# A hybrid RG-LRU and SSD step on one core: first chunk without an incoming state, a fourth new state in a norm bank, an earlier branch output, and a tail in two pieces

## The chip, the cores and the metric

The kernel runs on 1 core of a Trainium2 chip, as one launch. The metric is device microseconds of one execution, taken as the median over runs. A single profiled execution of the kernel before gives all the rows below.

## The reference, cut to what matters

One layer over 640 tokens (512 of a new stream, and 8 running streams of 16 tokens), model width 1024, all in fp32:

```python
x = x + 0.5 * swiglu_1(rmsnorm(x))
u = rmsnorm(x)
P = u @ w_in        # lru_x | lru_gate | ssd_z | ssd_xBC | ssd_dt | gates
a = lru_branch(P) @ w_br_lru                    # conv, RG-LRU scan, GeLU gate
# SSD branch, per group g of 4 (8 heads of 64, state 128), in chunks:
y_diag   = (C B^T * Lmat) @ (x * dt)            # inside a chunk
states_k = decay * states_(k-1) + B^T @ (decay_states * x * dt)
y        = y_diag + (C @ states_in) * exp(A_cs) + D * x   # new streams start from states = 0
b = (rmsnorm_group(y * silu(z))) @ w_br_ssd
x = x + (sigmoid(gA) * a + sigmoid(gB) * b) @ w_out
x = x + 0.5 * swiglu_2(rmsnorm(x))
return rmsnorm(x, norm_final_g), the new conv tails, LRU states and SSD states
```

## The kernel before, in words

The activations lie transposed, features on the partitions: 8 tiles of 128 features by 640 tokens, in two halves of 320 columns. Tokens form five chunks of 128: t = 0 to 3 are the prompt, t = 4 the sampled tokens. Each fp32 product is made of three products of a high and a low part. A **unit** is one 128-wide column tile of a weight matrix: 8 feature tiles x 3 products x 2 halves = 48 matmuls of 128x320 (36 in the last FFN group, which has 6 tiles). For each unit SyncE loads w_raw, ScalarE makes w_hi (`cut_weights`, L1005), VectorE makes w_lo (L1433), and TensorE (`unit`, `products`, L656) sums into pu[0] or pu[1], which alternate by a running number: `open_out(o)` waits until output o-2 has been read ("released") by its reader, mostly VectorE. Two more pairs of banks, pn[0] and pn[1], serve the norms and the SSD work.

Nothing schedules this but the order in the text, one loop per engine; the table FILL and `mixer_order()` give each unit of the mixer its place and number. For each SSD group g = 0..3: four units of x, B or C ("xb"), then for each prompt chunk t: `scores(t)` (transposes of x and B, and C B^T, into pn[0]), a unit beside it, `inner(t)` (L858: xd times lmat), the product with the state that comes in, ht (L876), the chunk's own state (L880, pn[1]), and units behind it. Units named z, gl, gs, bl and br are gates and branch projections; a br unit has two outputs, m = 0 and 1.

After chunk 3 comes the end of the group. TensorE transposes the prompt's state (L886, pn[1]), makes scores(4), one unit (`beside_last`), the old states' transposes (`old_state`, L899, pn[1]), inner(4), then four new sampled states, `new_state(0..3)` (L929: xdd times b_seq), with the units `middle` and `late` between 0, 1 and 2, and the products from the old states (`from_state`, L911) inside those units. All four new states use pu slots and numbers of the running order.

The other engines at that place. ScalarE: `decays(4)` (L1286, exp of lmat), then the prompt state's copy hp_rows (L1311) with its DMA (L1313), then b_tok (L1301), then the units. VectorE: the scan that makes lmat (L1853, `step_sums`), `scores(4)` (cbm L1860, xd L1862, xdd L1863, lmat L1866), then in groups 1 to 3 the second output of the last br unit (L1783 in group 1, L1789 and L1791 in group 2, L1794 in group 3) behind a w_lo cut, the beside_last unit's gate (L1763), later decay_states(1) (L1922), the middle unit, and the late unit's gate gbuf (L1427, or L1750 in group 0), and the adds of the new states (L1930). In groups 1 to 3 the late unit's gate reads gbuf, fetched from gate_spill by a ScalarE DMA (L1224). GpSimd: loads es and da_rep (L545, L551), clears ht, and makes b_seq from b_tok once the hp_rows DMA is done, because the two share memory (L599).

For t = 0 of a prompt group, ht is all zeros, cleared by GpSimd; VectorE multiplies the product with ht by es, adds the inner product, scales ht, and adds the chunk's state (L1874, L1876, L1879, L1883).

The decay sums before the mixer take 10 matmuls of 128x32 (L784, L787) and one of 128x128 (L789).

The tail. VectorE adds the last unit to resid (L1427), ScalarE squares it (L1016), VectorE adds the square to rvar (L1448). TensorE turns resid into rows of tokens by a matmul with a diagonal of the gains, `to_rows` (L969, g_fin), 8 for a chunk, and makes the sum of squares per token (L984). VectorE forms variance and scale (L2033 to L2039, with the root on ScalarE, L1416). Rows leave the banks by ScalarE for t = 0, 2, 4 (L1420) and by VectorE for t = 1, 3 (L2042); SyncE stores each chunk with one DMA of 512 KB (L433).

Of the kernel before, what the change touches and what calls it, by code (L numbers as in the profile page):

```python
# [68 lines left out]
def mixer_order():  # L69
# [3 lines left out]
    for g in range(GROUPS):  # L73
# [14 lines left out]
        yield ("new", g, 3), 0, 1  # L88
# [48 lines left out]
ES_PER = ((NT + 1) // 2 * 32, NT // 2 * 32)  # L137
# [10 lines left out]
dt_v dt_a dt_p after_v da_in0 da_in1 xb_th xb_out z_th ht_zero ssd_p ssd_a ssd_v bseq  # L148
h0_in0 h0_in1 hs_step old_mm old_cp c_split fs_mm fs_cp hs_out0 hs_out1 hp_mm hp_cp hp_out yz yn_hi_done yn_lo_done br_s gl_th gl_out0 gl_out1 gl_in gs_th gs_out
ma_in0 ma_in1 ma_in2 ma_in3 mg_b mg_v mh_done ml_done reload tail_mm tail_cp tails_out gfin fin_a fin_v y_a y_v y_dma""".split()  # L150
# [22 lines left out]
def layer(nc, x_prompt, x_sample, state_lru_conv, state_lru_h, state_ssd_conv, state_ssd_h,  # L173
# [7 lines left out]
    with ctx:  # L181
# [57 lines left out]
        with ExitStack() as sc:  # L239
# [14 lines left out]
            g_fin = sb(sc, "g_fin", [P, KT, P])  # L254
            y_out = sb(sc, "y_out", [P, NT, D_MODEL])
            fin = sb(sc, "fin", [P, 8, NT])

# [62 lines left out]
        fin_at = (pn[1], pu[O_FIN % 2], pu[(O_FIN + 1) % 2], pn[0], pn[1])  # L320
# [23 lines left out]
        def _(sp):  # L344
# [93 lines left out]
        def _(pool):  # L438
# [101 lines left out]
            for g in range(GROUPS):  # L540
# [99 lines left out]
        def _(pe):  # L640
# [36 lines left out]
            def ffn(u, o, ci, x_hi, x_lo, mid_hi, mid_lo, xh0, between, after):  # L677

                cut = ("xh_done", "xl_done", xh0, 0)
                for gi, n, uu, ou, cc, ud, od in ffn_plan(u, o, ci):  # L680
# [15 lines left out]
                    with pe.Fori(0, KT // 2) as i:  # L696
                        for k in range(2):
                            unit(ud + k, od + k, 2, 2, i, mid_hi, mid_lo, n, ready=hidden if k == 0 else None)

# [86 lines left out]
            for t in range(NT):  # L786
                pe.matmul(pn[1][:, 1, (NT + t) * HEADS:(NT + t + 1) * HEADS], le_mask[:, t // (NT - 1), :], da_col[:, t, :],  # L787
                          start=True, stop=True)
# [43 lines left out]
            for g in range(GROUPS):  # L832
# [20 lines left out]
                def inner(t):  # L853
# [6 lines left out]
                    ins.then_inc(s["ssd_p"], 1)  # L860
# [8 lines left out]
                for t in range(NT - 1):  # L869
# [3 lines left out]
                    if t == 0:  # L873
                        pe.wait_ge(s["ht_zero"], g + 1)
# [1199 lines left out]
```

## Time and profile before

| | |
|---|---|
| median of 3 runs | 1873.62 us (1873.21 to 1874.85) |
| the profiled execution | 1874.83 us |
| its span | 1873.1 us |
| TensorE clock granted, mean | 0.996 |
| TensorE busy | 1842.6 us, 98% |
| VectorE, ScalarE, GpSimd busy | 1111.5, 650.2, 141.1 us |

The span is what the profiler saw of the core; 1.7 us of the execution lie around it. TensorE executes nearly all the time, so the views to read are those that show where it does not (its waits by releaser), what runs on it that need not (timeline), and the end, where it has no work left. Each row of a timeline has the start in us, the duration of the (merged) instructions, the engine, the line, the operation, out<-in, the shape and a count; in brackets stands the engine's idle time before it and what ended it.

### The profile page before, as it was taken

How to read it: one execution, taken by the hardware profiler on the slowest of the kernel's cores; microseconds unless marked ns; L12 is line 12 of the kernel's file. 1: busy time of each engine (PE TensorE's matmuls, PEld its weight loads, DVE VectorE, ACT ScalarE, POOL GpSimd, SP SyncE). 2: the span in 40 equal slices, each digit the busy share in tenths (PEclk: the TensorE clock that was granted, in tenths of full speed). 3: DMA queues.
4: the chain of work that ended last, by engine and by line, in shares of the span. 5: the costliest groups of instructions: out<-in, count | busy, mean ns of one | idle time of the engine just before them, and what ended most of it. 6: DMA issues, size and time to landing. Idle time of an engine off the chain costs nothing.

```text
span 1873.1 us, 31253 instructions
## 1 busy us (share of the span) xinstructions
PE 1842.6 (98%) x12623; PEld 1791.3 (96%) x12623; DVE 1111.5 (59%) x1368; ACT 650.2 (35%) x850; POOL 141.1 (8%) x269
## 2 busy tenths in 40 slices
PE   8999999999999999999999999999999999999998
PEld 7999999999989999989989989998999999999998
DVE  6443443345777775777787887886754433442444
ACT  5221332123577742344244235233342212221223
POOL 3000000000011220111111101110200000000000
PEclk9999999999999999999999999999999999999999
DMA  5222222222422253353354335336522222222222
GB/s 148 68 78 73 73 78 71 76 78 59 135 63 80 70 145 110 110 173 92 112 152 119 107 98 168 106 107 214 191 67 79 78 79 68 78 79 68 78 65 81
DMA packets 273342, 186.13 MB, mean 99 GB/s; under 512 B 7452, under 2 KB 260580, under 8 KB 273008
## 3 DMA queue, kind: packets, MB, share of 16 engines
q1 hardware_dynamic: 239840, 129.52, 24.0%
q0 software_dynamic: 10624, 36.91, 6.5%
q10 hardware_dynamic: 22800, 18.62, 3.1%
q8 instruction: 55, 0.90, 0.2%
q14 instruction: 23, 0.19, 0.0%
HBM read 162.48 MB, written 22.53 MB: 99 GB/s over the span
## 4 chain that ended last, share of the span: by engine, by line
PE 86%; DVE 7%; ACT 3%; issue 2%; DMA 1%; ACTq 0%; DVEq 0%
PE pu L656 80%; DMA gbuf<-gate_spill 1%; PE pn L858 1%; PE pn L876 1%; DVE w_lo L1433 1%; PE pn L753 1%; PE pn L880 1%; PE pu L715 0%; DVE bc L1427 0%; PE pn L899 0%; DVE h_b L1922 0%; PE pn L911 0%; PE pn L847 0%; ACT w_hi L1005 0%; DVE squares L1427 0%
## 5 line engine op out<-in xcount | busy, mean ns | idle before, releaser
L1433 DVE TENSOR_TENSOR w_lo<-w_raw,w_hi 128x1024 fp32r<-128x1024 f32 x240 | 296.5, 1235 | 460.3 <-ACT w_hi L1005 458.7
L656 PE MATMUL pu<-act_hi,w_hi 128*128 128x320 f32 x1952 | 456.9, 315 | 6.7 <-DVE xc L1427 2.2
L656 PE MATMUL pu<-act_lo,w_hi 128*128 128x320 f32 x1952 | 446.9, 310 | 1.1 <-DVE act_lo L1476 1.0
L656 PE MATMUL pu<-act_hi,w_lo 128*128 128x320 f32 x1952 | 446.4, 310 | 0.0
L1005 ACT ACTIVATE w_hi<-w_raw 128x1024 fp32r<-128x1024 f32 x240 | 253.5, 1056 | 513.8 <-PE pu L656 512.7
L656 PEld LDWEIGHTS pu<-act_hi,w_hi 128*128 128x128 f32 x1952 | 327.0, 189 | 23.7 <-issue 19.6
L656 PE MATMUL pu<-x_hi,w_hi 128*128 128x320 f32 x1440 | 329.3, 310 | 1.3 <-DVE ff_g L1489 1.3
L656 PEld LDWEIGHTS pu<-act_lo,w_hi 128*128 128x128 f32 x1952 | 328.1, 189 | 2.4 <-DVE act_lo L1476 1.5
L656 PE MATMUL pu<-x_lo,w_hi 128*128 128x320 f32 x1440 | 328.4, 309 | 0.0
L656 PE MATMUL pu<-x_hi,w_lo 128*128 128x320 f32 x1440 | 328.4, 309 | 0.0
L656 PEld LDWEIGHTS pu<-act_hi,w_lo 128*128 128x128 f32 x1952 | 328.3, 189 | 0.0
L656 PEld LDWEIGHTS pu<-x_hi,w_hi 128*128 128x128 f32 x1440 | 240.8, 188 | 2.3 <-DVE ff_g L1489 1.8
L656 PEld LDWEIGHTS pu<-x_lo,w_hi 128*128 128x128 f32 x1440 | 240.7, 188 | 0.0
L656 PEld LDWEIGHTS pu<-x_hi,w_lo 128*128 128x128 f32 x1440 | 240.7, 188 | 0.0
L1286 ACT ACTIVATE lmat<-lmat 128x1024 f32<-128x1024 f32 x20 | 21.2, 1060 | 138.4 <-DVE lmat L1853 138.4
L1044 ACT ACTIVATE act_hi<-ff_h 128x640 f32 (+1 forms) x44 | 32.5, 739 | 94.3 <-DVE ff_h L1496 94.3
L1041 ACT ACTIVATE ff_t<-ff_g 128x640 f32<-128x640 f32 x44 | 32.5, 739 | 92.5 <-DVE ff_g L1489 92.5
L656 PE MATMUL pu<-yn_hi,w_hi 128*128 128x320 f32 x256 | 62.6, 326 | 0.2
L1498 DVE TENSOR_TENSOR act_lo<-ff_h,act_hi 128x640 f32 (+1 forms) x44 | 36.3, 825 | 44.5 <-ACT act_hi L1044 44.5
L656 PE MATMUL pu<-yn_lo,w_hi 128*128 128x320 f32 x256 | 58.4, 310 | 0.0
L656 PE MATMUL pu<-yn_hi,w_lo 128*128 128x320 f32 x256 | 58.2, 309 | 0.0
L1427 DVE SCALAR_TENSOR_TENSOR ff_a<-ff_t,ff_g 128x640 f32<-128x640 f32 x44 | 36.3, 825 | 35.4 <-ACT ff_t L1041 35.4
(323 smaller groups left out, 1883.9 us busy)
## 6 DMA issues: line engine op xcount, KB each, us to landing
w_raw<-in_ffn_w_up_dram SPq DMA_DIRECT2D x87, 512.0 KB, 3.8
w_raw<-in_w_in_dram SPq DMA_DIRECT2D x73, 512.0 KB, 3.9
w_raw<-in_ffn_w_down_dram SPq DMA_DIRECT2D x32, 512.0 KB, 3.7
da_rep<-e_spill POOLq DMA_DIRECT2D x20, 512.0 KB, 4.4
w_raw<-in_w_br_ssd_dram SPq DMA_DIRECT2D x16, 512.0 KB, 3.5
w_raw<-in_ffn_w_down_dram SPq DMA_DIRECT2D x16, 384.0 KB, 3.2
gate_spill<-gbuf ACTq DMA_DIRECT2D x18, 320.0 KB, 2.4
es<-e_spill POOLq DMA_DIRECT2D x40, 128.0 KB, 3.9
```

The costliest lines, as they stand in the source:

```text
L656: ins = pe.matmul(dst[:, h, :], w[:, side, c, :], a[:, k, h * HALF:(h + 1) * HALF], start=(at == 0), stop=(at == n - 1))
L753: ins = pe.matmul(pn[w][:, h, 0:HALF], w_gates[:, w, :], xc[:, h * HALF:(h + 1) * HALF], start=True, stop=True)
L858: ins = pe.matmul(pn[0][r:r + HD, 0, (h // 2) * P:(h // 2 + 1) * P], xd[:, h, :], lmat[:, h, :], start=True, stop=True)
L876: ins = pe.matmul(pn[0][:, 1, q * P:(q + 1) * P], ht[:, 2 * q:2 * q + 2, :].rearrange("n a b -> n (a b)"), xft(g, 5)[:, t * P:(t + 1) * P] ...
L880: pe.matmul(pn[1][:, 1, :], b_tok[:, :], xdd[:, :, :].rearrange("p h d -> p (h d)"), start=True, stop=True).then_inc(s["ssd_p"], 1)
L1005: act.activation(w_hi[:, side, :, :], w_raw[:, side, :, :], ACT.Copy).then_inc(s["w_hi_done"], 1)
L1041: act.activation(ff_t[:, :], ff_g[:, :], ACT.Tanh, scale=0.5).then_inc(s["ff_th"], 1)
L1044: act.activation(feature_tile(mid_hi, i), ff_h[:, :], ACT.Copy).then_inc(s["ff_hi"], 1)
L1286: act.activation(lmat[:, :, :], lmat[:, :, :], ACT.Exp).then_inc(s["ssd_a"], 1)
L1427: return dve.scalar_tensor_tensor(out=dst, in0=a, scalar=scalar, in1=b, op0=op0, op1=op1)
L1433: dve.tensor_tensor(w_lo[:, side, :, :], w_raw[:, side, :, :], w_hi[:, side, :, :].bitcast(F32), ALU.subtract).then_inc(s["w_lo_done"], 1)
L1498: dve.tensor_tensor(feature_tile(mid_lo, i), ff_h[:, :], feature_tile(mid_hi, i).bitcast(F32), ALU.subtract).then_inc(s["ff_lo"], 1)
```

## The change

Six parts. (1) new_state(3) goes into pn[1], with semaphores of its own (ns_mm, ns_v), and its number leaves the running order, so the next unit opens on the late unit's release. (2) At t = 0 TensorE leaves out the matmuls with ht; VectorE copies the inner product to es and the chunk's state to ht; GpSimd no longer clears ht or loads es for t = 0. (3) The decay sums are taken for four chunks in one matmul of 128x128. (4) ScalarE makes the last b_tok ahead of hp_rows and its DMA. (5) VectorE reads the br unit's second output ahead of scores(4), with the w_lo cut behind scores(4), in groups 1 to 3; decay_states(1) goes behind the middle unit and new_state(1). (6) The tail: the last down unit is summed by halves of 320 tokens; ScalarE multiplies resid by the gain as the units arrive (x_gain), so `to_rows` is a transpose and g_fin is gone; the sums of squares, variance, root and scale are made in two pieces (t = 0, 1 and t = 2, 3, 4); ScalarE takes out t = 0, 1, 3 and half of 4, VectorE t = 2 and the other half of 4; the last chunk is stored by two DMAs of 256 KB.

```diff
@@ mixer_order
-        yield ("new", g, 3), 0, 1
@@ tail banks
-        fin_at = (pn[1], pu[O_FIN % 2], pu[(O_FIN + 1) % 2], pn[0], pn[1])
+        fin_at = (pn[1], pu[O_FIN % 2], pn[0], pu[(O_FIN - 1) % 2], pn[1])
+        fin_sums = pu[(O_FIN - 1) % 2][:, 0, HALF:HALF + NT]
@@ SyncE: the last stores
-            for t in range(NT):
-                sp.wait_ge(s["y_v" if t % 2 else "y_a"], t // 2 + 1)
...
+            for t, name, n in ((0, "y_a", 1), (1, "y_a", 2), (2, "y_v", 1), (3, "y_a", 3)):
...
+            for b, name, n in ((0, "y_a", 4), (1, "y_v", 2)):
+                sp.wait_ge(s[name], n)
+                sp.dma_start(y_sample.rearrange("b l d -> (b l) d")[:, b * 512:(b + 1) * 512],
+                             y_out[:, NT - 1, b * 512:(b + 1) * 512]).then_inc(s["y_dma"], 16)
@@ GpSimd, start of a group
-                load_decay(0)
-                pool.memset(ht[:, :, :], 0.0).then_inc(s["ht_zero"], 1)
@@ TensorE: FFN, last down group
-                    with pe.Fori(0, KT // 2) as i:
+                    last = u == U_FFN2 and gi == len(FFN_GROUPS) - 1
+                    with pe.Fori(0, KT // 2 - (1 if last else 0)) as i:
...
+                    if last:
+                        unit(ud + KT - 2, od + KT - 2, 0, 0, 0, mid_hi, mid_lo, n)
+                        last_unit(ud + KT - 1, od + KT - 1, mid_hi, mid_lo, n)
+            def last_unit(u, o, hi, lo, nk):
...
+                for h in range(2):
+                    for k in range(nk):
+                        if h == 1 and k == nk - 1:
+                            token_sums(0)
+                        for w, a in ((w_hi, hi), (w_lo, hi), (w_hi, lo)):
+                            ins = pe.matmul(out(o)[:, h, :], w[:, u % 2, k, :], a[:, k, h * HALF:(h + 1) * HALF],
...
+                    ins.then_inc(s["out_ready" if h else "fin_half"], 1)
@@ TensorE: decay sums
-            for t in range(NT):
-                pe.matmul(pn[1][:, 0, t * HEADS:(t + 1) * HEADS], gt_mask[:, t // (NT - 1), :], da_col[:, t, :],
...
+            for m, chunks in enumerate((slice(0, NT - 1), slice(NT - 1, NT))):
...
@@ TensorE: SSD chunk loop
-                    if t == 0:
-                        pe.wait_ge(s["ht_zero"], g + 1)
-                    for q in range(PAIRS):
-                        ins = pe.matmul(pn[0][:, 1, q * P:(q + 1) * P],
...
+                    if t:
+                        for q in range(PAIRS):
+                            ins = pe.matmul(pn[0][:, 1, q * P:(q + 1) * P],
...
+                    if g and t == 0:
+                        pe.wait_ge(s["ns_v"], g)
@@ TensorE: new_state
-                    o = O_AT["new", g, q]
-                    open_out(o)
+                    if q < PAIRS - 1:
+                        open_out(O_AT["new", g, q])
+                        dst = pu[O_AT["new", g, q] % 2]
+                    else:
+                        dst = pn[1]
...
+                    ins.then_inc(s["out_ready" if q < PAIRS - 1 else "ns_mm"], 1)
@@ TensorE: tail
-            def to_rows(t, k):
-                return pe.matmul(fin_at[t][:, k // 4, (k % 4) * P:(k % 4 + 1) * P], resid[:, k, t * P:(t + 1) * P], g_fin[:, k, :],
...
+            def to_rows(t):
+                for k in range(KT):
+                    ins = pe.transpose(fin_at[t][:, k // 4, (k % 4) * P:(k % 4 + 1) * P], x_gain[:, k, t * P:(t + 1) * P], ident[:, :])
...
+            pe.wait_ge(s["fin_g"], KT)
+            to_rows(0)
+            pe.wait_ge(s["out_free"], O_FIN - 1)
+            to_rows(1)
+            token_sums(1)
+            pe.wait_ge(s["fin_g"], KT + 1)
+            to_rows(2)
+            pe.wait_ge(s["out_free"], O_FIN)
+            pe.wait_ge(s["fin_v"], 6)
+            to_rows(3)
+            pe.wait_ge(s["y_a"], 1)
+            to_rows(4)
@@ ScalarE: last unit by halves, after one x_gain tile with each earlier square
+                        for h in range(2):
...
+                            if h == 0:
+                                act.wait_ge(s["fin_r"], 1)
+                            else:
+                                token_root(0)
+                                act.wait_ge(s["out_free"], O_FIN)
+                            act.activation(squares[:, 1, part], resid[:, KT - 1, part], ACT.Square).then_inc(s["fin_sq"], 1)
+                            act.activation(x_gain[:, KT - 1, part], resid[:, KT - 1, part], ACT.Copy,
...
@@ ScalarE: chunk loop (the four lines of hp_rows move up, behind the last b_tok)
+                    if t == NT - 1:
+                        act.wait_ge(s["hp_mm"], g + 1)
+                        act.activation(hp_rows[:, :, :].rearrange("p q n -> p (q n)"), pn[1][:, 1, :], ACT.Copy).then_inc(s["hp_cp"], 1)
...
-                    if t == NT - 2:
...
@@ ScalarE: tail
+            rows_out(0, 2)
+            token_root(1)
+            rows_out(1, 2)
+            rows_out(3, 2)
+            rows_out(4, 1)
@@ VectorE: outputs of a chunk
+                    if t:
+                        decay_in(t)
...
+                    else:
...
+                        dve.tensor_copy(yv, pn[0][:, 0, :]).then_inc(s["ssd_v"], SV_T2 - SV_G)
...
+                        dve.tensor_copy(hv, pn[1][:, 1, :]).then_inc(s["ssd_v"], SV_H1 - SV_T2)
@@ VectorE: end of a group
-                scores(NT - 1)
-                finish(held[0])
+                if held[0][0] == "br":
+                    branch_out(*held[0][1:], 1, cut=False)
+                    scores(NT - 1)
+                    branch_cut(*held[0][1:])
+                else:
+                    scores(NT - 1)
+                    finish(held[0])
...
-                decay_states(1)
                 fill([middle])
                 new_state(1)
+                decay_states(1)
```

VectorE at the end of group 1, before: the scan, then the four operations of scores(4), a weight cut, and only then the second output of the br unit, acc_ssd.

```order
L1783 TENSOR_TENSOR acc_ssd<-rstd,pu 128x640
L1853 SCALAR_TENSOR_TENSOR lmat<-da_rep,after 128x1024
L1860 TENSOR_TENSOR cbm<-pn,le_mask 128x128
L1862 TENSOR_TENSOR xd<-pn,dt_col 128x512
L1863 TENSOR_TENSOR xdd<-pn,dd_col 128x512
L1866 TENSOR_TENSOR lmat<-lmat,cbm 128x1024
L1433 TENSOR_TENSOR w_lo<-w_raw,w_hi 128x1024
L1783 TENSOR_TENSOR acc_ssd<-rstd,pu 128x640
L1763 TENSOR_SCALAR gbuf<-gbuf 128x640
```

The same place in the changed kernel:

```order
L1861 TENSOR_TENSOR acc_ssd<-rstd,pu 128x640
L1931 SCALAR_TENSOR_TENSOR lmat<-da_rep,after 128x1024
L1861 TENSOR_TENSOR acc_ssd<-rstd,pu 128x640
L1938 TENSOR_TENSOR cbm<-pn,le_mask 128x128
L1940 TENSOR_TENSOR xd<-pn,dt_col 128x512
L1941 TENSOR_TENSOR xdd<-pn,dd_col 128x512
L1944 TENSOR_TENSOR lmat<-lmat,cbm 128x1024
L1481 TENSOR_TENSOR w_lo<-w_raw,w_hi 128x1024
L1838 TENSOR_SCALAR gbuf<-gbuf 128x640
```

The second acc_ssd has moved from behind the cut to ahead of cbm; the cut stays behind scores(4).

TensorE behind the last down unit, before: 7 of the 8 row matmuls of chunks 0 and 1, the last of each, then the sums per token (ones, rvar) inside chunk 2.

```order
L969 MATMUL pn<-g_fin,resid 128x128 x7
L969 MATMUL pu<-g_fin,resid 128x128 x7
L969 MATMUL pn<-g_fin,resid 128x128
L969 MATMUL pu<-g_fin,resid 128x128 x5
L984 MATMUL pn<-ones,rvar 128x1 x5
L969 MATMUL pu<-g_fin,resid 128x128 x4
L969 MATMUL pn<-g_fin,resid 128x128 x16
```

The same place in the changed kernel, from the last feature tile of the second half on:

```order
L709 MATMUL pu<-ones,rvar 128x1 x2
L721 MATMUL pu<-act_hi,w_hi 128x320
L721 MATMUL pu<-act_hi,w_lo 128x320
L721 MATMUL pu<-act_lo,w_hi 128x320
L1000 MATMUL pn<-ident,x_gain 128x128 x8
L1000 MATMUL pu<-ident,x_gain 128x128 x8
L709 MATMUL pu<-ones,rvar 128x1 x3
L1000 MATMUL pn<-ident,x_gain 128x128 x8
L1000 MATMUL pu<-ident,x_gain 128x128 x8
L1000 MATMUL pn<-ident,x_gain 128x128 x8
```

Two of the sums now stand inside the last unit, three behind the rows of chunks 0 and 1.

## Rows read from the trace of the kernel before

**Rows 1.** The page, part 1: busy time, share of the span and instructions.
```profile
PE 1842.6 (98%) x12623; PEld 1791.3 (96%) x12623; DVE 1111.5 (59%) x1368; ACT 650.2 (35%) x850; POOL 141.1 (8%) x269
```

**Rows 2.** TensorE's waits: who waited <- for whom: us in total, times, longest.
```profile
PE pu L929 <- DVE gbuf L1427: 2.9, 3, 1.1
...
PE pu L929 <- DVE squares L1789: 1.6, 1, 1.6
PE pu L656 <- DVE gbuf L1763: 1.6, 3, 0.5
...
PE pu L656 <- DVE gbuf L1750: 1.2, 2, 0.8
...
PE pn L899 <- ACT h_t L1325: 0.8, 2, 0.4
PE pu L929 <- DVE acc_ssd L1783: 0.8, 1, 0.8
...
PE pu L656 <- DVE h_b L1930: 0.4, 1, 0.4
```

**Rows 3.** Chain of waits, last 39 us of TensorE's units: start, us, what.
```profile
1818.96 37.52 PE pu L656 x254
```

**Rows 4.** Timeline of TensorE, first chunk of group 1.
```profile
873.95 1.16 PE L876 MATMUL pn<-bc,ht 128*128 128x128 f32 x8
874.94 0.59 PE L880 MATMUL pn<-xdd,b_tok 128*128 128x512 f32 x1
```

**Rows 5.** Timeline of TensorE, the end of group 2.
```profile
1099.14 1.09 PE L858 MATMUL pn<-lmat,xd 128*64 128x128 f32 x16
1101.85 1.13 PE L929 MATMUL pu<-b_seq,xdd 64*128 64x512 f32 x4 [1.61 <-DVE squares L1789]
...
1127.07 1.13 PE L929 MATMUL pu<-b_seq,xdd 64*128 64x512 f32 x4 [0.72 <-DVE gbuf L1427]
```

**Rows 6.** Timeline of VectorE, the end of group 2.
```profile
1091.68 2.28 DVE L1853 TENSOR_TENSOR_SCAN lmat<-da_rep,after 128x1024 f32<-128x1024 f32 x1
1096.38 0.29 DVE L1860 TENSOR_TENSOR cbm<-pn,le_mask 128x128 f32<-128x128 f32 x1 [2.41 <-ACT b_tok L1301]
...
1098.91 2.06 DVE L1433 TENSOR_TENSOR w_lo<-w_raw,w_hi 128x1024 fp32r<-128x1024 f32 x1
1100.90 0.81 DVE L1789 TENSOR_TENSOR squares<-rstd,pu 128x640 f32<-128x640 f32 x1
```

**Rows 7.** Timeline of ScalarE and GpSimd, the end of group 2.
```profile
1094.96 0.58 ACT L1311 ACTIVATE hp_rows<-pn 128x512 f32<-128x512 f32 x1
...
1095.99 0.28 ACT L1301 ACTIVATE b_tok<-pn 128x128 f32<-128x128 f32 x1 [0.46 <-ACT hp_rows L1311]
...
1097.93 1.96 POOL L599 TENSOR_TENSOR b_seq<-b_tok,half_mask 128x512 f32<-128x512 f32 x1 [15.77 <-DMA out_dram<-hp_rows]
```

**Rows 8.** Timeline of TensorE, the decay sums.
```profile
547.83 1.20 PE L784 MATMUL pn<-da_col,gt_mask 128*128 128x32 f32 x10
...
550.62 0.53 PE L656 MATMUL pu<-act_hi,w_hi 128*128 128x320 f32 x2 [0.18 <-DVE g_t L1427]
```

**Rows 9.** Timeline of all engines, the tail.
```profile
1856.59 0.82 DVE L1427 SCALAR_TENSOR_TENSOR resid<-pu,resid 128x640 f32<-128x640 f32 x1 [2.89 <-PE pu L656]
1857.45 0.74 ACT L1016 ACTIVATE squares<-resid 128x640 f32<-128x640 f32 x1 [4.61 <-DVE resid L1427]
...
1863.75 1.11 ACT L1420 ACTIVATE y_out<-pn,fin 128x1024 f32<-128x1024 f32 x1 [1.19 <-DVE fin L2039]
...
1864.89 4.16 SPq L433 DMA_DIRECT2D out_dram<-y_out  x5
```

**Rows 10.** The five stores of the tail, by their line: issue to landing.
```profile
DMA to landing us min/median/max: 2.7/4.3/4.9
```

**Rows 11.** Bytes moved, 1864.9 to 1872.8 us, in 40 equal slices.
```profile
GB/s 0 0 0 0 311 394 436 394 415 353 456 373 436 394 353 477 394 374 394 456 373 456 373 394 415 373 436 373 415 415 394 394 415 456 394 394 373 21 0 0
```

**Rows 12.** Timeline of VectorE, the late unit's gate of group 1.
```profile
972.23 0.82 DVE L1427 SCALAR_TENSOR_TENSOR gbuf<-pu,gbuf 128x640 f32<-128x640 f32 x1 [1.40 <-DMA gbuf<-gate_spill]
```

More of the change, by code:

```diff
@@ L782, in _ @@
             pe.wait_ge(s["lru_a"], LA + LA_TI)
-            for t in range(NT):
-                pe.matmul(pn[1][:, 0, t * HEADS:(t + 1) * HEADS], gt_mask[:, t // (NT - 1), :], da_col[:, t, :],
+            for m, chunks in enumerate((slice(0, NT - 1), slice(NT - 1, NT))):
+                cols = slice(chunks.start * HEADS, chunks.stop * HEADS)
+                pe.matmul(pn[1][:, 0, cols], gt_mask[:, m, :], da_col[:, chunks, :].rearrange("p t h -> p (t h)"),
                           start=True, stop=True)
-            for t in range(NT):
-                pe.matmul(pn[1][:, 1, (NT + t) * HEADS:(NT + t + 1) * HEADS], le_mask[:, t // (NT - 1), :], da_col[:, t, :],
-                          start=True, stop=True)
+                pe.matmul(pn[1][:, 1, NT * HEADS:2 * NT * HEADS][:, cols], le_mask[:, m, :],
+                          da_col[:, chunks, :].rearrange("p t h -> p (t h)"), start=True, stop=True)
             pe.matmul(pn[1][:, 1, 0:(NT - 1) * HEADS], ones[:, :],
@@ L1052, in ffn @@
                     last = final and gi == len(FFN_GROUPS) - 1
+                    if last:
+                        act.wait_ge(s["tails_out"], 16 * TAIL_DMAS)
                     with act.Fori(0, KT // 2 - (1 if last else 0)) as i:
@@ L1528, in ffn, with token_var, token_scale @@
                     if last:
-                        for k in range(2):
-                            down(KT // 2 - 1, k, False)
+                        down(KT // 2 - 1, 0, False)
+                        for h in range(2):
+                            part = slice(h * HALF, (h + 1) * HALF)
+                            r = resid[:, KT - 1, part]
+                            if h == 0:
+                                dve.wait_ge(s["fin_half"], 1)
+                                stt(r, out(O_FIN - 1)[:, h, :], 0.25, r, ALU.mult, ALU.add).then_inc(s["fin_r"], 1)
+                            else:
+                                dve.wait_ge(s["out_ready"], O_FIN)
+                                stt(r, out(O_FIN - 1)[:, h, :], 0.25, r, ALU.mult, ALU.add).then_inc(s["out_free"], 1)
+                                token_scale(0)
+                            dve.wait_ge(s["fin_sq"], h + 1)
+                            dve.tensor_tensor(rvar[:, part], rvar[:, part], squares[:, 1, part], ALU.add).then_inc(s["fin_add"], 1)
+                            token_var(h)
+            def token_var(part):
+                cols = (slice(0, 2), slice(2, NT))[part]
+                dve.wait_ge(s["fin_sum"], part + 1)
+                chained("fin_v", 5 * part, dve.tensor_scalar(fin[:, 1, cols], fin_sums[:, cols], 1.0 / D_MODEL, EPS, ALU.mult, ALU.add), 1)
+            def token_scale(part):
+                f = [fin[:, k, (slice(0, 2), slice(2, NT))[part]] for k in range(6)]
+                dve.wait_ge(s["fin_a"], part + 1)
+                chained("fin_v", 5 * part, dve.reciprocal(f[3], f[2]), 2)
+                chained("fin_v", 5 * part, dve.tensor_tensor(f[4], f[1], f[3], ALU.mult), 3)
+                chained("fin_v", 5 * part, stt(f[4], f[4], -0.5, f[3], ALU.mult, ALU.mult), 4)
+                chained("fin_v", 5 * part, stt(f[5], f[4], 1.5, f[3], ALU.add, ALU.mult), 5)
             def chained(name, base, ins, j):
@@ L1771, in silu_z, with branch_cut, branch_out @@
                 cut_behind(("z", g, q))
-            def branch_out(g, r, m):
+            def branch_cut(g, r):
+                cut_weights(U_AT["br", g, r] + 2, 0, 0)
+            def branch_out(g, r, m, cut=True):
                 o = O_AT["br", g, r] + m
-                if m == 1:
-                    cut_weights(U_AT["br", g, r] + 2, 0, 0)
+                if m == 1 and cut:
+                    branch_cut(g, r)
                 dve.wait_ge(s["out_ready"], o + 1)
```

143 lines of the change are left out of this document (67 added, 76 removed).

## The prediction

> **What bounds the kernel now.** I read the page's busy line first: TensorE executes for 98% of the span [rows 1]. Time can therefore only be won in two ways: work that TensorE need not do, or stretches in which it stands. TensorE's waits by releaser come next [rows 2]. No single wait is large, but seven groups of rows lie at the ends of the SSD groups, where the new states and the late unit compete for two pu slots. Third is the last stretch of the chain of waits, an unbroken run of 254 matmuls that begins at 1818.96 and takes 37.52 us, so one per 0.148 us [rows 3]. It ends at 1856.48, and the span at 1873.1: a tail of 16.6 us in which TensorE no longer sets the time. Last are timelines at the places that the change edits. The tail's stores move bytes without a gap [rows 11], so the tail ends when the first store could start, plus five stores.
>
> **The change part by part.**
>
> *First chunk.* The eight records with ht start at 873.95 and the next matmul starts at 874.94 [rows 4]: 0.99 us, four times, **4.0 us**. They lie between two other TensorE operations without a wait, so all of it should be seen. The bounds are 3.0, if inner(0) then meets something late in one group, and 4.0. VectorE loses two of four operations, GpSimd a clearing and two loads; none of them is waited for in rows 2, so I count them as nothing. Their cover is a whole unit: 48 x 0.148 = 7.1 us by rows 3.
>
> *Fourth new state in pn[1].* Today it waits for the late unit's gate: 2.9 us in three groups [rows 2]. In the second group of rows 5 TensorE starts it at 1127.07 after 0.72 idle. It no longer needs a pu slot. The next unit does need that release, but stands behind both new states, which take about 1.1 us each [rows 5], so the release has come when it is reached (in no group did it come later than 1.1 us after new_state(2)). In group 0 the same slot order shows as 1.2 us for the bl unit's gate, of which I take 1.0, and 0.4 for h_b, the add of a new state. Together **4.3 us**; bounds 2.9 (the first row alone) and 4.5.
>
> *Branch output, b_tok and decay_states.* Before, VectorE waits 2.41 us for b_tok ahead of cbm, while b_tok waits on ScalarE for hp_rows and the issue of its DMA [rows 6, 7]. The branch's second output comes behind scores(4) and two weight cuts, at 1100.90, and new_state(0) waits 1.61 us for it [rows 5, 6]; group 1 loses 0.8 in the same way [rows 2]. Now the two operations of some 0.82 us stand where VectorE was idle, from the scan's end at 1091.68 + 2.28 = 1093.96 to about 1095.6. b_tok moves ahead of hp_rows, by 1095.99 - 94.96 = 1.0 us, to about 1095.0 to 1095.3. So cbm starts at about 1095.7 instead of 1096.38, and inner(4), which TensorE reaches at 1099.14, is not later. What is late next is b_seq: its DMA goes out about 0.3 us later, so b_seq ends at 1097.93 + 1.96 + 0.3 = 1100.2, where inner(4) ends too (1099.14 + 1.09) [rows 5, 7]. I leave 0.2 us for that: 1.6 + 0.8 - 0.2 = **2.2 us**. Bounds: 0.7, if hp_rows and its DMA come a whole 1.5 us later in both groups, and 2.4. Of the old states' wait for ScalarE's h_t [rows 2] I take half, **0.4**; bounds 0 and 0.8. The gate L1763 hangs on the unit just ended and stays.
>
> *Decay sums.* Twenty records become eight. Ten cost 1.20 us [rows 8], so TensorE is free about 1.1 us sooner. But the next unit was already released by VectorE's g_t, 0.18 us after TensorE was free [rows 8], and VectorE does nothing sooner. I count **0**; the upper bound is 1.1.
>
> *Tail.* Before: from the last unit's end, 1856.48, to VectorE's add, ScalarE's square, the sums, the scale chain, rows out at 1863.75, first store at 1864.89 [rows 9], then to the end: 16.6 us. After, with zero at the end of the first half: half a unit is 18 x 0.148 = 2.7 us. VectorE's add of 320 columns ends at 0.6 (0.82 us for 640 [rows 9], so some 0.47), square 1.1, gain 1.55, rvar 1.6; the first sums run at 2.2 inside the second half without a wait. The second half ends at 2.7 + 0.6 for the sums = 3.3. VectorE adds at 3.4 to 3.9 and makes the first scale by 4.7. TensorE transposes chunks 0 and 1 at 3.3 to 5.2, and sums the rest until 6.0. Rows of chunk 0 leave on ScalarE at 4.9 to 6.0, chunk 1 at 6.7 to 7.8. The store of chunk 0 could start at 6.1, but the queue is then short until chunk 1 comes at 7.8. From there, 1.4 us until bytes move (the first store took 2.7 to land [rows 10], 1.3 of it for its 512 KB: about 400 GB/s [rows 11]), then four times 1.3, to 14.4, and 0.35 to the end of the span as before: 14.75. Less 2.7 for the half that was TensorE's in any case, 12.1 against 16.6: **4.4 us**. Bounds: 3.0, if ScalarE's root stands behind chunk 0's rows and chunk 1 comes 1.4 later, and 5.2, if chunk 0's store hides a further 0.8. ScalarE's extra multiply, one per unit of 5.3 us, is covered: a 128x640 operation takes 0.74 [rows 9].
>
> Five or six stores with a fixed part each would end later than this. The rows speak against it: 512 KB land every 1.3 us with no slice empty between [rows 11], so the fixed part of one lies beside the bytes of another. The Trainium skill ("DMA: Bandwidth & Descriptors", section "Anatomy of one DMA — SWDGE (gpsimd) path") gives a DMA about 2.0 us fixed, whatever its size, plus bytes at 436 GB/s, for another path than SyncE's queue; by it one more DMA could cost 2.0, and the time would be an estimated 1860.3. The stores here show it only for the first of them.
>
> **Sum.** 4.0 + 4.3 + 2.2 + 0.4 + 0 + 4.4 = 15.3 us. The profiled execution took 1874.83, so it would take 1859.5. It is 1.2 above the median of the runs, 1873.62, so my number against the median is **1858.3**. The bounds sum to 10.3 to 18.4 if all fell on one side, 1855.2 to 1863.3.
>
> **The rivals.**
>
> *The waits come back.* TensorE reaches every later operation at the group ends sooner, and VectorE's work there is not shorter. If the waits of rows 2 reappear at the next units, only the first chunk and the tail remain: 4.0 + 4.4 = 8.4, **1865.2**. For it: VectorE and ScalarE are busy in these stretches. Against: VectorE itself waits 2.41 us there [rows 6].
>
> *A fixed cost for each queued store.* The last two half stores come one behind the other; if the extra one costs 1.4 us, **1859.7**. Rows 11 speak against it.
>
> *The branch reorder does nothing.* If cbm slips behind the branch output as far as new_state(0) gains, the 2.2 go: **1860.5**. That is the case in which this part does not do what it says; the slack of inner(4) speaks against it.
>
> *The decay sums show after all:* VectorE's g_t is sooner by as much, **1857.2**.
>
> *Slower.* In groups 1 to 3 the next group's first unit, or the unit gl 6 after the last, now opens straight on the late unit's release, and VectorE's gate there waits for a fetch: 1.40 us in group 1 [rows 12]. If the fetches landed later than now, nothing would stand between. With 15.3 us won, the three places would each have to lose 15.3 / 3 + 1.1 = 6.2 us before the kernel is slower; at 7 us each, 1.1 us of cover taken off, 17.7 lost: **1876.0**. Against it: the fetch is issued by ScalarE behind b_tok, which moves earlier, with the hp_rows DMA alone put ahead of it.
>
> **How the numbers follow.** About 0.2%, 3.7 us, is what a measurement of this kernel can tell from no change. My forecast 0.76, waits come back 0.10, store cost 0.06, reorder does nothing 0.04, decay sums 0.02, slower 0.02. All but the last are faster by over 3.7 us, the nearest by 8.4: faster 0.96. I give 0.02 to no change, taken from the waits' case, should the tail's bytes not start sooner as well, and 0.02 to slower. The range is the bounds', cut where all terms fall low together: **1855.0 to 1862.8**. It takes in the store cost, the reorder and the decay sums, and leaves out the waits' case and slower.
>
> **What would show it.** Right: no L876-like matmul in the first chunk and inner(0) followed at once by the state matmul; no wait of a new state's matmul for gbuf or for the branch's output; waits of pu units for gbuf no longer than before; a b_seq wait under 0.3 us; TensorE's last unit to the span's end in about 12 us, and bytes without a gap from chunk 1's store on. Wrong: a new row of TensorE's waits over 1 us at the group ends, for b_seq, gbuf or xd; a gap between stores; or a last unit whose second half waits for the sums of the first.

## The result and the profile after

| | before | changed |
|---|---|---|
| median | 1874.23 us (1873.21 to 1875.62, 4 runs) | 1860.92 us (1860.33 to 1864.48, 4 runs) |
| ratio, 95% interval | | 0.9932 [0.9915, 0.995] |
| profiled execution | 1874.83 us | 1860.66 us |
| span | 1873.1 us | 1858.9 us |

The change is 13.3 us faster by the medians, and 14.2 by the two profiles. The forecast was 15.3 us and 1858.3, with a range of 1855.0 to 1862.8: the range holds, the number was 2.6 us too low. The medians of this document leave out the few executions that took far longer than the others of their kernel.

The page's first part now, beside [rows 1]:

```profile
PE 1831.9 (99%) x12539; PEld 1782.0 (96%) x12539; DVE 1103.3 (59%) x1358; ACT 656.6 (35%) x862; POOL 133.7 (7%) x257
```

TensorE's waits by releaser in the changed kernel (total, times, longest; the waits at the very start are left out):

```profile
PE pu L657 <- DVE w_lo L1481: 1.9, 2, 1.3
PE pu L657 <- DVE g_t L1475: 1.7, 2, 1.5
PE pu L657 <- DVE gbuf L1838: 1.6, 3, 0.5
...
PE pu L657 <- DVE gbuf L1475: 0.7, 1, 0.7
PE pu L958 <- POOL b_seq L600: 0.7, 1, 0.7
...
PE pn L925 <- ACT h_t L1366: 0.4, 1, 0.4
```

Against [rows 2]: the new states wait no longer for the gate or for the branch output. Four rows are new or longer: w_lo (before 0.7, once), g_t behind the decay sums (1.5), gbuf L1475, which now stops a unit, and b_seq.

Where the time went is read by following the same matmul through two profiles. The table counts TensorE's lead over the kernel before, from the first unit behind the decay sums on (so the spread of the first 550 us is left out), as the difference of the starts of the same instruction. One loss stands in no row: with part 2 alone 1.3 us between that unit and group 0's first chunk, a spell at the lower clock (last section). Columns: the changed kernel; then the experiments below.

| us gained in | changed | part 2 alone | part 1 alone | parts 4, 5 alone | part 6 alone |
|---|---|---|---|---|---|
| first chunk, each group | 0.9 | 0.9 | 0 | 0 | 0 |
| end of group 0 | 1.8 | 0 | 0.6 | 1.25 | 0 |
| end of group 1 | 1.5 | -0.4 | 1.1 | 0.4 | -0.2 |
| end of group 2 | 2.4 | 0 | 1.1 | 2.4 | 0 |
| group 3 to its first br unit | 0.3 | -1.5 | -0.4 | 0.1 | -0.5 |
| from there to the end (tail) | 5.1 | 0 | 0 | -0.3 | 5.1 |

For the changed kernel the sum is 4 x 0.9 + 1.8 + 1.5 + 2.4 + 0.3 + 5.1 = 14.7 us. Ahead of the first unit behind the decay sums the changed kernel's profile lost 0.4 (551.01 against 550.62), which leaves about the 14.2 of the two profiles; these lie further apart than the medians.

### The profile page after: what moved, and what is told of

Read it like the earlier page. It is cut to its first block, busy times and chain, and to the rows that moved or that the text cites. A ratio compares the mean times of both kernels' runs of the same rounds, so it can differ in the third digit from the quotient of the medians.

```text
span 1858.9 us, 31067 instructions
## 1 busy us (share of the span) xinstructions
PE 1831.9 (99%) x12539; PEld 1782.0 (96%) x12539; DVE 1103.3 (59%) x1358; ACT 656.6 (35%) x862; POOL 133.7 (7%) x257
## 4 chain that ended last, share of the span: by engine, by line
PE 88%; DVE 5%; ACT 2%; issue 2%; DMA 2%; ACTq 0%; DVEq 0%; POOL 0%; SPq 0%; POOLq 0%
PE pu L657 81%; PE pn L883 1%; PE pn L778 1%; PE pn L906 1%; PE pn L925 1%; PE pn L900 1%; DVE w_lo L1481 1%; DMA gbuf<-gate_spill 1%; PE pu L740 0%; DVE bc L1475 0%; DMA gate_spill<-gbuf 0%; PE pn L872 0%; ACT w_hi L1023 0%; PE pu L958 0%; PE pn L937 0%
## 5 line engine op out<-in xcount | busy, mean ns | idle before, releaser
L1475 DVE SCALAR_TENSOR_TENSOR ff_a<-ff_t,ff_g 128x640 f32<-128x640 f32 x44 | 36.3, 825 | 35.4 <-ACT ff_t L1059 35.4
```

The source lines that it names most:

```text
L1475: return dve.scalar_tensor_tensor(out=dst, in0=a, scalar=scalar, in1=b, op0=op0, op1=op1)
```

## Experiments

Times are medians; the kernel before ran beside each on the same chip (1873.55, 1873.11 and 1873.05 us in the three sets).

### Each part alone

**Part 2**, kernel before with

```diff
-                    for q in range(PAIRS):
-                        ins = pe.matmul(pn[0][:, 1, q * P:(q + 1) * P],
+                    if t:
+                        for q in range(PAIRS):
+                            ins = pe.matmul(pn[0][:, 1, q * P:(q + 1) * P],
...
-                load_decay(0)
-                pool.memset(ht[:, :, :], 0.0).then_inc(s["ht_zero"], 1)
```

and VectorE's two copies at t = 0.

> The kernel before with part 2 alone (no matmul with the zero state, no clearing, no es load at t = 0; two copies on VectorE). Theory A, each part gains what its own place in the trace shows: 3.6 us (0.90 in each of the four groups, since the state matmul's first record then starts 0.1 later), so about 1870.6 against 1874.2. Rival: the whole 0.99 us shows, 4.0, or the time comes back as longer waits at the group ends (gain under 2).

Measured: 1870.47 us, 3.1 less, ratio 0.9985 [0.9976, 0.9994].

**Part 1**, kernel before with

```diff
-                    o = O_AT["new", g, q]
-                    open_out(o)
+                    if q < PAIRS - 1:
+                        open_out(O_AT["new", g, q])
+                        dst = pu[O_AT["new", g, q] % 2]
+                    else:
+                        dst = pn[1]
```

> The kernel before with part 1 alone (fourth new state in pn[1]). Theory A: 4.1 us at the group ends (1.6 in group 0, 0.4, 0.8 and 1.2 in groups 1 to 3), less a new wait of TensorE for w_lo of about 1.2 us at the first br unit of group 3 if that wait comes from TensorE reaching this place sooner than the weight loads do: 2.9 to 4.1. Rival: that w_lo wait was an accident of the profiled run and doesn't come here (TensorE <- w_lo total 0.7 to 0.8 as before), gain 4.1 or more.

Measured: 1871.01 us, 2.5 less, ratio 0.9985 [0.9976, 0.9993].

**Parts 4 and 5**, kernel before with the hp_rows lines behind b_tok and

```diff
-                scores(NT - 1)
-                finish(held[0])
+                    branch_out(*held[0][1:], 1, cut=False)
+                    scores(NT - 1)
+                    branch_cut(*held[0][1:])
...
-                decay_states(1)
                 fill([middle])
                 new_state(1)
+                decay_states(1)
```

> The kernel before with parts 4 and 5 alone (b_tok ahead of hp_rows, branch output ahead of scores(4), decay_states(1) later). Theory A: 0.8 in group 1 and 0.95 in group 2 at new_state(0), and 0.5 to 0.7 in group 2 at the old states' transpose: 1.8 to 2.5 us. A wait for b_seq of about 0.7 in group 2. Rival: with new_state(3) still behind the gate, the time won at new_state(0) is lost again at new_state(3): gain under 1.

Measured: 1869.35 us, 4.2 less, ratio 0.9979 [0.9969, 0.9988].

**Part 6**, kernel before with the whole tail of the changed kernel (unit by halves, x_gain, two pieces, stores).

> The kernel before with part 6 alone (tail in two pieces). Theory A: 5.0 us as the profiles show from the last unit's end to the span's end, everything ahead of it unchanged. Rival: the ScalarE gain per unit (0.81 us each) or the smaller stores cost something of it: 4.0 to 4.4.

Measured: 1867.98 us, 5.6 less, ratio 0.9972 [0.996, 0.9983].

The sum of the four is 15.4 us, and the whole change gave 13.3: no part is eaten whole by another. The leads of the table add up to 2.4 with part 1 alone, 3.8 with parts 4 and 5 and 4.4 with part 6, against 2.5, 4.2 and 5.6 by the medians. With part 2 alone they give 1.7 and the median 3.1: its profiled execution, at 1873.30 us, was the slowest of twelve, and lost 1.5 in group 3. The waits of TensorE with part 2 alone, and then with part 1 alone:

```profile
PE pu L926 <- DVE gbuf L1424: 2.9, 3, 1.5
...
PE pu L654 <- DVE w_lo L1430: 2.6, 2, 2.0
```

```profile
PE pu L655 <- DVE w_lo L1441: 2.2, 2, 1.6
...
PE pu L655 <- DVE gbuf L1758: 1.2, 2, 0.8
...
PE pu L655 <- DVE gbuf L1435: 0.4, 1, 0.4
```

Two things follow. The w_lo row is not new with the whole change: it is there with either part, and with the tail, which edits nothing ahead of it (0.5 us in the table). And group 0's wait for the bl gate, 1.2 us, is untouched by part 1: with parts 4 and 5 it is gone, and new_state(3) still waits for the gate, 2.5 us:

```profile
PE pu L929 <- DVE gbuf L1427: 2.5, 3, 1.0
...
PE pn L899 <- ACT h_t L1325: 0.4, 1, 0.4
```

Against what was expected: part 2 came out at 0.9 us in each group, as theory A said, though the median's 3.1 has an interval too wide to tell 3.6 from 4.0. Part 1 gave less than its 2.9 to 4.1, because group 0 gave 0.6 where 1.6 was expected. Parts 4 and 5 gave 4.2 where 1.8 to 2.5 was expected: group 0's 1.25 was not in it, and group 2 gave 2.4 instead of 1.5 to 1.7. Their rival (lost again at new_state(3)) fell, and the expected b_seq wait did not come. For part 6 the trace gives 5.1 at the tail, as expected; the interval of its median (3.2 to 7.5 us) does not exclude the rival's 4.0 to 4.4.

### Parts 4 and 5 undone one by one

b_tok behind hp_rows again:

> The changed kernel with part 4 undone (hp_rows and its DMA ahead of the last b_tok again). Theory A, as the forecast had it: cbm is covered by the branch output that now stands ahead of it, so little is lost at inner(4); the b_seq wait of 0.7 in group 2 goes, and 0.5 in group 0 (no br output there) comes back: within 0.5 us of the changed kernel. Rival: the earlier b_tok carries the gain, and TensorE's inner(4) waits for VectorE: 1.5 us or more slower than the changed kernel.

Measured: 1861.9 us.

The branch output behind scores(4) again:

> The changed kernel with the branch output behind scores(4) again. Theory A: new_state(0) waits for it again in groups 1 and 2, 1.8 to 2.4 us slower than the changed kernel (1860.9). Rival: with the earlier b_tok VectorE reaches the branch output 0.7 sooner, so only about 1.0 to 1.3 comes back.

Measured: 1861.21 us.

decay_states(1) ahead of the middle unit again:

> The changed kernel with decay_states(1) ahead of the middle unit again. Theory A: in group 0 TensorE waits 0.8 us again for the middle bl unit's copy, nothing in groups 1 to 3 where the gate L1838 hangs on ScalarE: 0.8 us slower than the changed kernel. Rival, as the forecast booked it: that wait went with part 1, so nothing changes (0.2 at most).

Measured: 1861.45 us.

The intervals (each about 0.0014 either way, 2.6 us) don't tell these apart from the changed kernel by time, so the table of leads decides:

| us gained in | changed | changed, again | no part 4 | no branch reorder | no decay reorder |
|---|---|---|---|---|---|
| end of group 0 | 1.8 | 1.8 | 1.4 | 1.8 | 1.0 |
| end of group 1 | 1.5 | 1.85 | 1.5 | 1.9 | 1.6 |
| end of group 2 | 2.4 | 2.05 | 1.3 | 1.75 | -0.6 |

The branch reorder is worth nothing in group 1, where without it TensorE has no wait for acc_ssd at new_state(0): the earlier b_tok brings VectorE there in time. That is the rival's way, and even less came back than its 1.0 to 1.3. In group 2 its 0.3 to 0.65 is mixed with the b_seq wait, which stands at 1.4 us there. The earlier b_tok gives 0.4 in group 0, and the run without it 0.7 to 1.1 less in group 2; its b_seq wait there is 1.26 us, not gone as theory A said. The later decay_states(1) gives 0.8 in group 0, as theory A said and against the forecast's booking. Its -0.6 in group 2 is another matter, told in the last section.

### The changed kernel again, and one store

> The changed kernel itself once more, beside the others on one chip. Theory A: the same parts within 0.3 us at the group ends; only the wait ahead of the first br unit (w_lo), the b_seq wait and the spells at the lower clock near 20, 520 and 550 us differ from run to run. Rival: a wait of over 1 us at another place, so that the first profile was not typical.

Measured: 1860.98 us, ratio 0.9934 [0.992, 0.9947]. The leads agree within 0.4 us at every place of the table; the b_seq wait was 1.0 and the one at the first br unit 1.2.

For the last chunk, one DMA instead of two:

```diff
-            for b, name, n in ((0, "y_a", 4), (1, "y_v", 2)):
-                sp.wait_ge(s[name], n)
-                sp.dma_start(y_sample.rearrange("b l d -> (b l) d")[:, b * 512:(b + 1) * 512],
...
+            sp.wait_ge(s["y_a"], 4)
+            sp.wait_ge(s["y_v"], 2)
+            sp.dma_start(y_sample.rearrange("b l d -> (b l) d"), y_out[:, NT - 1, :]).then_inc(s["y_dma"], 16)
```

> The changed kernel with the last chunk stored by one DMA of 512 KB instead of two of 256 KB. Theory A: the queue is full until the end, so the last bytes leave at the same time: within 0.3 us of the changed kernel. Rival, a fixed cost for each store: 1.4 us faster.

Measured: 1860.49 us; its tail gains 5.1 us over the kernel before, as the changed one's. The extra store costs nothing that can be seen, so the forecast's second rival falls. The Trainium skill ("DMA: Bandwidth & Descriptors", section "Anatomy of one DMA — SWDGE (gpsimd) path") states a fixed part of about 2.0 us for each DMA on another path than SyncE's queue; by it one store less would have saved an estimated 2.0 us. For stores queued one behind the other on SyncE's queue the measurement decides: 0.4 to 0.5 by the medians, nothing in the tail.

### The new waits, taken away

They hang on DMAs. VectorE at the first br unit of group 3, and TensorE behind it, in the changed kernel:

```profile
1291.56 0.82 DVE L1475 SCALAR_TENSOR_TENSOR gbuf<-pu,gbuf 128x640 f32<-128x640 f32 x1 [3.27 <-DMA gbuf<-gate_spill]
1292.30 1.22 DVE L1481 TENSOR_TENSOR w_lo<-w_raw,w_hi 128x1024 fp32r<-128x1024 f32 x1
```

```profile
1293.57 0.56 PE L657 MATMUL pu<-yn_hi,w_hi 128*128 128x320 f32 x2 [1.26 <-DVE w_lo L1481]
```

VectorE at the same place in the kernel before, where the br unit started at 1302.80:

```profile
1300.79 0.82 DVE L1427 SCALAR_TENSOR_TENSOR gbuf<-pu,gbuf 128x640 f32<-128x640 f32 x1 [2.11 <-DMA gbuf<-gate_spill]
1301.53 1.22 DVE L1433 TENSOR_TENSOR w_lo<-w_raw,w_hi 128x1024 fp32r<-128x1024 f32 x1
```

The gate of gl 7 needs its fetch into gbuf, which needs gl 6's spill from the same gbuf to have landed; the weight cut that the br unit needs stands behind that gate on VectorE. First, gl 7 gets a tile that is dead by then:

```diff
+        gl_last = bc[:, 0, 0, :]
...
             fetch_branch(LAST_UNITS[0][1])
+            fetch_branch(LAST_UNITS[1][1])
```

> The changed kernel with a buffer of its own for the last gl unit's gate (a bc tile that is dead by then), fetched with the one of gl 6, so that this gate no longer waits for a spill to land and a fetch behind it. Theory A: TensorE's w_lo wait ahead of the first br unit of group 3 (1.26 in the changed kernel, 0.11 before, 0.7 to 2.0 in three of four variants) falls under 0.2: 0.8 to 1.5 us faster than the changed kernel, about 1859.7. Rival: the wait moves on to the next unit (yn_lo, or the gate of gs 7), gain under 0.3.

Measured: 1858.91 us, ratio 0.9922 [0.9908, 0.9935]. The stretch from group 3 to its first br unit gains 1.7 us instead of 0.3, and the w_lo row is 0.7, once, as before the change.

Second, the fetch of the late unit's gate, which ScalarE issued behind two 512 KB stores, goes ahead of them:

```diff
-                states_out(0)
                 if late[0] == "gl":
                     fetch_branch(late[1])
                 from_state_copy(1)
+                states_out(0)
```

> The changed kernel with the buffer of its own for the last gl unit, and with the fetch of the late unit's gate and the copy of the from-state rows issued ahead of the two stores of new states. Theory A: VectorE's gate in group 1 no longer waits for its fetch behind 1 MB of stores, TensorE's wait of 0.6 to 0.7 for it goes: about 0.6 us faster than the kernel with the buffer alone (median 1858.9 there). Rival: ScalarE, held by the wait for the spill ahead of the fetch, makes the from-state rows late and the time comes back there.

Measured: 1856.05 us, ratio 0.9913 [0.99, 0.9927]. The end of group 1 gains 2.3 us instead of 1.7 with the buffer alone. The median fell by 2.9 against that kernel; the leads account for 0.6 of it, and the two profiled executions lie 0.5 apart (1856.54 and 1856.05), so the rest is no more than the spread of the runs (1856.54 to 1860.36 with the buffer alone).

Third, hp_rows of groups 1 to 3 lie in rtmp, so b_seq no longer shares memory with a store under way:

```diff
+        def hp_at(g):
+            return rtmp[:, 0:PAIRS * NS].rearrange("p (q n) -> p q n", q=PAIRS) if g else hp_rows[:, :, :]
...
-                pool.wait_ge(s["hp_out"], g * 16 + 16)
+                if not g:
+                    pool.wait_ge(s["hp_out"], 16)
```

> As the kernel with the fetch first, and hp_rows in groups 1 to 3 in a buffer that is idle there (rtmp), so that b_seq no longer waits for the hp_rows store. Theory A: TensorE's wait for b_seq in group 2 (0.5 to 2.1 in five profiles) goes: 0.5 to 1.0 us faster than the kernel with the fetch first. Rival: new_state(0) then waits for the unit beside it instead, gain under 0.2.

Measured: 1855.15 us (1854.83 to 1855.99), ratio 0.9904 [0.9889, 0.9919]: 5.8 us below the changed kernel beside it, and the fastest here. The end of group 2 gains 3.5 us instead of 2.6. Its waits:

```profile
PE pu L663 <- DVE g_t L1487: 1.7, 2, 1.5
PE pu L663 <- DVE gbuf L1854: 1.6, 3, 0.5
...
PE pu L663 <- DVE w_lo L1493: 0.7, 1, 0.7
```

b_seq and the fetched gate are gone from the list.

## Why the prediction was right, and where it was not

**First chunk: 4.0 forecast, 3.6 measured.** The mechanism held; the step took the whole 0.99 of [rows 4], but of the state matmul's records the first now takes about 0.1 longer:

```profile
871.62 1.13 PE L906 MATMUL pn<-xdd,b_tok 128*128 128x512 f32 x2
872.18 0.86 PE L657 MATMUL pu<-act_hi,w_hi 128*128 128x320 f32 x2
```

From the first state record to the unit are 0.56 us; before, from 874.94 [rows 4], 0.46:

```profile
875.40 0.86 PE L656 MATMUL pu<-act_hi,w_hi 128*128 128x320 f32 x2
```

**Fourth new state: 4.3 forecast, of which 1.0 for group 0's bl gate; 3.9 measured without that gate** (0.6, 0.7, 1.1 and 1.5 in the four groups, from new_state(2) to the next state matmul less its own 0.9, and in group 3 to the br unit without its new wait). "The release has come when it is reached" failed in group 1:

```profile
966.85 1.13 PE L958 MATMUL pu<-b_seq,xdd 64*128 64x512 f32 x4
967.81 1.02 PE L958 MATMUL pn<-b_seq,xdd 64*128 64x512 f32 x4
969.58 0.53 PE L657 MATMUL pu<-act_hi,w_hi 128*128 128x320 f32 x2 [0.75 <-DVE gbuf L1475]
```

new_state(3) (pn) follows at once, as forecast, but the next unit waits 0.75 for the gate. This is the slower rival's mechanism, at its place, at a tenth of the price that it needed; the run with the fetch first removed it. And the 1.0 us booked for group 0's bl gate belongs to parts 4 and 5, as part 1 alone showed: that this term came out was luck, since another part paid it.

**Branch, b_tok and decay_states: 2.2 forecast for groups 1 and 2, 1.8 measured** (0.83 and 0.95 at new_state(0)), and the 1.2 of group 0 from above. Of the old states' wait 0.4 was forecast and 0.4 came, in group 2. "b_seq's DMA goes out about 0.3 us later" was nearly right (0.17 against TensorE's inner(4)), but its landing was taken as fixed, and b_seq came 0.67 late where the sum left 0.2. Bytes moved and the store's issue to landing around it, before (1091 to 1101 us) and after (1086 to 1096), 40 slices each:

```profile
GB/s 0 0 0 0 66 0 0 0 0 0 0 0 0 0 0 0 0 0 0 0 0 2 293 354 338 62 0 0 0 0 0 0 0 0 0 0 0 0 0 0
...
q8 instruction: 1, 0.02, 0.6%
...
out_dram<-hp_rows ACTq DMA_DIRECT2D x1, 256.0 KB, 2.2
```

```profile
GB/s 0 0 0 0 0 0 0 0 0 0 0 0 0 0 0 0 0 0 0 0 281 322 330 117 0 0 8 10 18 23 6 0 0 0 37 100 92 51 84 115
...
q10 hardware_dynamic: 528, 0.26, 8.9%
...
q8 instruction: 1, 0.02, 0.9%
...
out_dram<-hp_rows ACTq DMA_DIRECT2D x1, 256.0 KB, 3.9
```

Nearly all of the store's bytes take four slices, 1.0 us, in both. After the change the store reports its landing 1.7 us later, and the small numbers behind its four slices are its own last bytes. The DMA queues of the changed kernel from 1091.1 to 1092.1 us, then from 1092.1 to 1094.1, where nothing else moves:

```profile
q8 instruction: 1, 0.02, 9.2%
```

```profile
q10 hardware_dynamic: 33, 0.02, 3.5%
```

q10 is the queue of ScalarE's stores: 33 of its 528 packets, a sixteenth, come only between 1092.65 and 1093.6. With 16 DMA engines this reads as the share of one of them. q8 is the queue that the profile calls instruction, fetches of the program's own code: its one packet, of 16 KB, starts at 1091.18, 1.06 us behind the store's issue, and takes 1.48 us, to 1092.66, where the late sixteenth begins. Before, the packet of q8 (the 66 GB/s of the first row) was through 2.5 us ahead of the store's issue. SyncE's next weight load is not the cause: its bytes begin at 1094.65, and b_seq had started at 1094.19.

In group 2 of the five profiles of the kernel before and of single parts, b_seq started 2.4 us after the store's issue; in the eight with all parts, or all but one, and hp_rows in its old place, it was 3.7 to 4.6. In these eight, and in the one with hp_rows moved, an instruction fetch starts 1.06 to 1.12 us behind the store's issue, takes 1.2 to 1.9 us, and the store's last packet ends 3.1 to 4.0 us behind the issue. In the 47 other stores of hp_rows in the 14 profiles no instruction fetch overlaps the store, and the last packet ends at 1.8 to 2.1. That b_seq was freed of the late landing by moving hp_rows is shown; that the instruction fetch causes it is read from these rows and was not tried.

**Decay sums: 0, as forecast in the trace:** the unit is released by g_t at the same moment, and TensorE's wait for it grew from 0.18 to 1.54 us. What may hang on the longer wait stands in the last section.

**Tail: 4.4 forecast, 5.1 measured.** The steps came in the forecast order, each a little sooner:

```profile
1844.73 0.49 DVE L1475 SCALAR_TENSOR_TENSOR resid<-pu,resid 128x320 f32<-128x320 f32 x1 [0.19 <-PE pu L721]
...
1849.17 1.09 ACT L1462 ACTIVATE y_out<-pn,fin 128x1024 f32<-128x1024 f32 x1
...
1850.29 3.58 SPq L432 DMA_DIRECT2D out_dram<-y_out  x4
...
1850.72 1.10 ACT L1462 ACTIVATE y_out<-pu,fin 128x1024 f32<-128x1024 f32 x1
...
1853.94 2.10 SPq L435 DMA_DIRECT2D out_dram<-y_out  x2
```

Chunk 1 left ScalarE at 1851.82, 7.2 us after the first half's end (some 1844.6), where the sum had 7.8. This step was over-priced by 0.6.

**What the sum did not have at all: 1.15 us at the first br unit of group 3.** The forecast looked at the gates that wait for a fetch in groups 1 to 3 and gave them 0.02 as a slower rival; it did not look at the same chain behind the last group, gl 7's fetch and the weight cut behind its gate, where before the change no slack was left (VectorE already waited 2.11 us for that fetch in the kernel before, TensorE 0.11 for w_lo). From the spill's issue to the gate were 6.6 us before and with parts 4 and 5 alone, 7.7 in the changed kernel, 7.2 with part 6 alone, 8.0 and 8.4 with parts 1 and 2 alone. The DMA queues in that stretch, before (1294.23 to 1300.79 us) and after (1283.84 to 1291.56), show this difference:

```profile
q0 software_dynamic: 97, 0.41, 15.8%
```

```profile
q0 software_dynamic: 235, 1.04, 35.2%
```

q0 carries GpSimd's four loads of merged. Their first was issued 7.4 to 7.5 us ahead of the spill before, with parts 4 and 5 alone and with part 6 alone, and q0 moved 0.35 to 0.41 MB in the stretch; with parts 1 and 2 alone and in the changed kernel it was 5.9 to 6.2 us, and 0.86 to 1.04 MB. So the spill, coming sooner, runs beside more of these loads. An instruction fetch also falls into the stretch in all but the two fastest. Which of the two makes the transfers longer was not tried; that the chain set the time is shown by the run that cut it.

Step by step: 15.3 - 0.4 (first chunk) + 0.6 (fourth state: 3.9 instead of 3.3) + 0.2 (bl gate: 1.2 instead of 1.0) - 0.4 (branch and b_tok) + 0.7 (tail) - 1.15 (first br unit) = 14.85, near the 14.7 that the leads show. The terms were 1.5 too low and 1.95 too high in all, so that the sum came this near is in part luck. The first rival, waits that come back at the group ends, was right in kind at two places and for 1.4 us in all; the reorder rival was right in group 1, where the earlier b_tok had already paid. Of the signs that the forecast named, two failed: the b_seq wait is 0.67 instead of under 0.3, and a unit waits 0.75 for gbuf at a place where none did.

Two sums of the prediction are off. Its tail of 12.1 against 16.6 is 4.5 us, not 4.4. And the bounds of its terms add up to 9.6 to 18.0 us, 1855.6 to 1864.0, not to 10.3 to 18.4; the measured time lies inside either.

## What to carry to other kernels

When a wait behind a gate is removed, follow the gate's own inputs too: a buffer that must be spilled before it is fetched again, or that shares memory with a store under way, has slack that is gone as soon as the compute engine comes a microsecond sooner. A transfer's landing is not a constant to be carried from one profile to the next: look at what all the queues move around it, the instruction fetches too, and leave a wait on a store that other traffic can come to overlap a margin (1.3 to 2.2 us here). And ascribe a wait to a part only after reading what its releaser does ahead of it: group 0's bl gate waited for VectorE's backlog, not for the slot.

## What the runs showed of the hardware that was not expected

**Short spells at the lower clock.** TensorE's granted clock is 1.00 in nearly the whole span, but not behind some waits. In the kernel before, windows of 2 us (busy time and count by engine, then granted clock, DMA share, GB/s):

```profile
517.00:519.00 2.00, 0.00 (x0) 0.00 (x0) 1.65 (x2) 1.02 (x4) 0.21 (x1) 0.84 0.00 1
519.00:521.00 2.00, 1.84 (x7) 1.88 (x8) 1.93 (x4) 0.00 (x0) 0.00 (x0) 0.50 0.92 244
521.00:523.00 2.00, 2.00 (x9) 2.00 (x8) 0.10 (x2) 1.85 (x5) 0.00 (x0) 0.50 0.06 17
523.00:525.00 2.00, 2.00 (x9) 2.00 (x9) 1.97 (x3) 0.48 (x1) 0.00 (x0) 0.50 0.00 0
525.00:527.00 2.00, 2.00 (x10) 1.60 (x9) 0.47 (x1) 0.00 (x0) 0.00 (x0) 0.95 0.67 180
```

After a wait of 2.19 us TensorE runs at half clock, 1.2 GHz, for about 6 us. At the same place the mean over 515 to 530 us was 0.77 before, in the changed kernel and with part 1 alone, 0.89 in seven others and 1.00 in the three kernels with a buffer for gl 7 and the one with a single store, although the wait is the same: it differs from one execution to the next. Between the first unit and the one behind the decay sums, the profile with 1.00 of the kernel with gl 7's buffer was 2.7 us shorter than the kernel before. That is as large as many terms of the forecast, and may be part of the spread of the runs.

The kernel without the decay reorder shows it at a group's end, after a b_seq wait of 2.09 us. Its -0.6 in the table is 1.4 us of longer wait and 1.6 us of lower clock against the changed kernel's 2.4. TensorE's row, then windows:

```profile
1094.85 1.13 PE L958 MATMUL pu<-b_seq,xdd 64*128 64x512 f32 x4 [2.09 <-POOL b_seq L600]
```

```profile
1096.00:1097.50 1.50, 1.50 (x8) 1.46 (x9) 1.42 (x3) 0.00 (x0) 0.70 (x2) 0.64 1.09 336
1097.50:1099.00 1.50, 1.50 (x9) 1.50 (x9) 0.41 (x1) 0.00 (x0) 0.00 (x0) 0.50 0.23 67
```

In the kernel with one store a wait of 2.23 us at the first br unit of group 3 was followed by a granted clock of 0.52 and 0.63 over 1292 to 1296 us, and took another 1.5 us there; its tail is counted from behind that place.

**The decay sums may have a price after all.** In the second profile of the changed kernel the longer wait behind them is followed by the lower clock too:

```profile
549.42 0.70 PE L657 MATMUL pu<-act_hi,w_hi 128*128 128x320 f32 x2 [1.54 <-DVE g_t L1475]
```

```profile
549.40:551.40 2.00, 1.98 (x8) 2.00 (x9) 1.34 (x2) 2.00 (x5) 0.00 (x0) 0.56 0.06 12
551.40:553.40 2.00, 2.00 (x11) 2.00 (x10) 1.60 (x3) 1.98 (x4) 0.21 (x1) 0.59 0.01 3
```

It costs 1.3 us there (the lead at the next group is smaller by as much). Seven of nine profiles with part 3 show such a spell between 545 and 565 us, and one of the five without it. It also goes with the spell before it: the four profiles with a mean of 1.00 over 515 to 530 us all have it, the three with 0.77 do not, with part 3 or without. If part 3 brings it, the medians' 13.3 and 12.1 us against the leads' 14.7 would have part of their cause here; no run undid part 3, so this is left open.
